# Expert rows of a mixture-of-experts stage added to their tokens by TensorE in PSUM, nine expert buffers in place of seven

## The chip, the core and the metric

The kernel runs on one NeuronCore of a Trainium2 chip. The metric is the device time of one execution in microseconds (us), here the median of three runs of the same program. The profile is of a fourth execution, taken by the hardware profiler; its clock starts at the first instruction.

## What is computed

One decoder layer for T = 320 tokens (256 of a prompt, 64 = 8 sequences of 8 new tokens), width 1024, all in fp32. First a mixer (a convolution group and a state-space group side by side, then one output projection), then a mixture of experts, then a last RMSNorm. The change touches the mixture of experts and the end:

```
t   = rmsnorm(x)                                   # 320 rows of 1024
grp = argmax(t @ rg_w + rg_b)                      # one of 4 groups
top 2 of the group's 8 experts, weights g1 * softmax(top 2)
for e in range(32):
    hid = silu(t @ w_gate[e]) * (t @ w_up[e])      # w_gate, w_up: 1024 x 512
    acc = acc + combine[:, e:e+1] * (hid @ w_down[e])   # w_down: 512 x 1024
y   = rmsnorm(x + acc)
```

Each token goes to 2 of 32 experts, so an expert has 20 tokens on average (640 pairs of token and expert over 32). A weight matrix of an expert holds 2 MiB, an expert three of them, all 32 experts 96.

## The kernel before

Everything is written by hand with semaphores, engine by engine; no scheduler reorders it. `S("name")` is a semaphore, `wait_ge` a wait, `then_inc` the count that an instruction adds when it is done. SP (SyncE) issues all weight loads from one queue, in order. `ring` holds six 2 MiB buffers through which first the mixer's weights and then the experts' weights go.

**The experts' weights.** `expert_units` (line 61) lists the 96 matrices in the order gate 0, up 0, gate 1, up 1, down 0, gate 2, up 2, down 1, and so on to gate 31, up 31, down 30, down 31. They are called units here, numbered 0 to 95; up 31 is unit 93. `e_slot` (line 362) has seven buffers: the six of the ring and `last_gate`, a piece of region_b. Unit j goes to buffer j mod 7 and is issued (line 440) when the unit seven before it has been used: after `gu_done` (gate and up product of an expert finished) or `dn_done` (down product finished).

**Routing.** After the output projection, VectorE (DVE) ranks the experts, gives each pair of token and expert a slot (at most CAP = 64 slots per expert), and TensorE turns that into lists by slot with a small product of 0/1 matrices (`slot_values`, line 1054): `gidx` (which row to gather), `sidx` (where to scatter), `wsl` (the weight of the slot).

**The expert loop.** GpSimd gathers the rows of expert e from `hn_dram` (line 677) into `gat`, an indirect DMA. TensorE (PE) then does for each expert, in this order: `gate_up(e)`, 16 products of 128x64 by 128x512 in pairs (lines 1079 and 1080, gate to partitions 0 to 63 of a PSUM bank and up to 64 to 127); `tokens_T(e+1)`, 8 transposes of the next expert's rows (line 1069); `down(e-1)`, 8 products (line 1091); `hidden_T(e)`, 4 transposes (line 1085). ScalarE (ACT) takes silu (line 1350), DVE multiplies and copies (helper line 1386). Each of these four products has two PSUM banks of its own, by even and odd expert, so all eight banks are used. `weigh(e)` (DVE, line 1717) multiplies the 64 rows of an expert by their weights into `yo`; one 128x512 tile, rows 0 to 63 with columns 0 to 511 of the result and rows 64 to 127 with columns 512 to 1023.

**Back to the tokens.** GpSimd scatters `yo` to `ye_dram` (line 682), where each token has two places, one for its first and one for its second expert. When all scatters have landed, GpSimd counts `ye_all` (line 721), SP reloads the 320 tokens' rows of both experts into the ring (line 510), and DVE adds both to `xt` (`add_experts`, line 1386 by the helper). Then the last RMSNorm: square on ACT (line 1367), square root on ACT (line 1370), reciprocal on DVE (line 1765), scaling on DVE (line 1387 by the helper), output by SP (line 514).

A branch for more than 64 tokens in one expert exists on every engine; each engine reads `mcount` into a register (`value_load`) behind the loop and jumps over it.

## Time and profile before

| | us |
|---|---|
| median of 3 runs | 903.55 |
| the runs | 900.63, 903.55, 903.62 |
| the profiled execution | 905.3 |
| its span, first to last instruction | 903.5 |
| PE busy | 768.4 (85%) |
| DVE, ACT, POOL busy | 300.5, 116.8, 191.2 |
| DMA, all queues | 254.54 MB, 282 GB/s over the span |

### The profile page before, as it was taken

The page shows a single profiled execution, that of the slowest core. Times are in us where ns is not written, and L with a number is a line of the kernel's source. Part 1 is how long each engine was busy: PE and PEld are TensorE (multiplying, and loading weights), DVE is VectorE, ACT ScalarE, POOL GpSimd, SP SyncE. Part 2 cuts the span into 40 slices and gives each one's busy share as a digit, 9 for nine tenths or more (in the row PEclk, how much of TensorE's full clock was granted, in tenths as well). Part 3 has the DMA queues.
Part 4 walks back from the last instruction along what each step waited for, and adds up shares of the span by engine and source line. Part 5 has one row for each costly group of instructions (what it writes and reads, how often), then busy time and mean ns, then how long its engine had stood idle before and what let it go on. Part 6 is the DMA issues. An engine that isn't in the chain of part 4 may idle for free.

```text
span 903.5 us, 8844 instructions
## 1 busy us (share of the span) xinstructions
PE 768.4 (85%) x3474; PEld 388.6 (43%) x3474; DVE 300.5 (33%) x662; ACT 116.8 (13%) x247; POOL 191.2 (21%) x219
## 2 busy tenths in 40 slices
PE   4999999989999996599987988798797797977970
PEld 3777677777533335343333332333242332333320
DVE  2079999952666114411111110101111011110105
ACT  3200211245410011000000000000000000000002
POOL 2088997310020002011111110101110111111010
PEclk9999999999999996589999988998898999989995
DMA  9882300216072994059999999999999999999915
GB/s 276 323 297 95 110 1 1 67 34 187 24 240 62 296 398 175 3 207 403 420 422 407 419 414 418 401 426 416 397 415 407 408 417 425 407 420 411 399 47 174
DMA packets 53544, 254.54 MB, mean 282 GB/s; under 512 B 8993, under 2 KB 26433, under 8 KB 40879
## 3 DMA queue, kind: packets, MB, share of 16 engines
q1 hardware_dynamic: 44948, 245.37, 68.9%
q0 software_dynamic: 5264, 5.40, 2.0%
q10 hardware_dynamic: 3291, 3.20, 1.2%
q8 instruction: 28, 0.46, 0.2%
q14 instruction: 13, 0.11, 0.0%
HBM read 248.96 MB, written 17.00 MB: 294 GB/s over the span
## 4 chain that ended last, share of the span: by engine, by line
PE 83%; issue 9%; DVE 5%; ACT 2%; DMA 1%; POOLq 0%; ACTq 0%; SPq 0%; DVEq 0%
PE bank L1079 27%; PE bank L744 18%; PE bank L1091 13%; PE bank L996 8%; PE bank L1069 4%; PE bank L1085 2%; PE bank L1080 1%; DVE region_a L1386 1%; PE bank L1041 1%; PE bank L826 1%; PE bank L969 1%; DMA ring<-ye_scratch 1%; PE bank L985 1%; PE bank L960 1%; DVE xt L1386 1%
## 5 line engine op out<-in xcount | busy, mean ns | idle before, releaser
L1079 PE MATMUL bank<-ring,region_a 128*64 128x512 f32 x432 | 216.9, 661 | 53.5 <-issue 52.6
L1080 PE MATMUL bank<-ring,region_a 128*64 128x512 f32 x432 | 217.5, 662 | 0.0
L744 PE MATMUL bank<-region_a,ring 128*128 128x320 f32 x576 | 158.9, 437 | 0.5 <-DVE region_a L1386 0.5
L1079 PEld LDWEIGHTS bank<-ring,region_a 128*64 128x64 f32 x432 | 63.1, 152 | 176.8 <-issue 176.3
L1386 DVE TENSOR_TENSOR zz<-zz,bank 64x512 f32<-64x512 f32 x32 | 22.1, 690 | 341.1 <-ACT zz L1350 341.1
L744 PEld LDWEIGHTS bank<-region_a,ring 128*128 128x128 f32 x576 | 109.9, 192 | 46.6 <-issue 2.1
L1091 PE MATMUL bank<-ring,region_a 128*64 128x512 f32 x448 | 102.3, 598 | 0.5 <-issue 0.5
L1387 DVE SCALAR_TENSOR_TENSOR bank<-region_a,par,bank 128x256 f32<-128x256 f32 x232 | 91.2, 481 | 0.0
L1080 PEld LDWEIGHTS bank<-ring,region_a 128*64 128x64 f32 x432 | 63.2, 152 | 0.0
L682 POOL DMA_INDIRECT ye_scratch<-yt,region_a x32 | 32.4, 1014 | 145.1 <-DVE yt L1717 141.3
L1350 ACT ACTIVATE zz<-bank 64x512 f32<-64x512 f32 x32 | 18.9, 592 | 335.5 <-PE bank L1080 335.5
L677 POOL DMA_INDIRECT vv<-hn_scratch,region_a x16 | 15.4, 963 | 194.4 <-PE bank L1069 168.6
L1079 PE MATMUL bank<-region_b,region_a 128*64 128x512 f32 x80 | 40.0, 657 | 15.4 <-issue 15.3
L1091 PEld LDWEIGHTS bank<-ring,region_a 128*64 128x64 f32 x448 | 30.2, 136 | 50.5 <-issue 48.8
L1717 DVE TENSOR_SCALAR yt<-bank,region_a 128x512 f32<-128x512 f32 x32 | 24.0, 750 | 83.6 <-PE bank L1091 83.6
L677 POOL DMA_INDIRECT yt<-hn_scratch,region_a x15 | 14.3, 956 | 126.0 <-PE bank L1069 126.0
L1080 PE MATMUL bank<-region_b,region_a 128*64 128x512 f32 x80 | 39.8, 656 | 0.0
L996 PE MATMUL bank<-ring,yt 128*128 128x512 f32 (+1 forms) x96 | 37.9, 603 | 0.0
L996 PE MATMUL bank<-ring,vv 128*128 128x512 f32 (+1 forms) x96 | 37.6, 608 | 0.0
L578 POOL TENSOR_TENSOR xt<-xt 128x512 f32<-128x512 f32 x29 | 36.8, 1269 | 2.3
L576 POOL TENSOR_TENSOR xt<-region_a,par 128x512 f32<-128x512 f32 x30 | 32.3, 1077 | 1.9
L1353 ACT ACTIVATE region_a<-bank 128x256 f32<-128x256 f32 x32 | 12.3, 384 | 144.0 <-PE bank L1085 144.0
(302 smaller groups left out, 699.0 us busy)
## 6 DMA issues: line engine op xcount, KB each, us to landing
ring<-in_expert_w_down SPq DMA_DIRECT2D x28, 2048.0 KB, 27.8
ring<-in_expert_w_gate SPq DMA_DIRECT2D x27, 2048.0 KB, 28.4
ring<-in_expert_w_up SPq DMA_DIRECT2D x27, 2048.0 KB, 23.1
ring<-in_w_in SPq DMA_DIRECT2D x9, 2048.0 KB, 20.2
region_b<-in_expert_w_gate SPq DMA_DIRECT2D x5, 2048.0 KB, 29.7
region_b<-in_expert_w_up SPq DMA_DIRECT2D x5, 2048.0 KB, 22.8
ring<-in_w_out SPq DMA_DIRECT2D x4, 2048.0 KB, 9.1
region_b<-in_expert_w_down SPq DMA_DIRECT2D x4, 2048.0 KB, 28.4
```

The source lines that it names most:

```text
L576: link(pool.tensor_tensor(tmp4, u_seq[:, :, :, k:k + TB], w4(par, k, NC), ALU.mult))
L578: return link(pool.tensor_tensor(acc, acc, tmp4, ALU.add))
L677: pool.indirect_dma_start(gat[e % 2], None, hn_dram[:, :], bass.IndirectOffsetOnAxis(ap=gidx[0:CAP, e:e + 1], axis=0), bounds_check=T - 1, ...
L682: pool.indirect_dma_start(ye_dram[:, :], bass.IndirectOffsetOnAxis(ap=sidx[:, e:e + 1], axis=0), yo[e % 2], None, bounds_check=4 * T - 1, ...
L744: ins = pe.matmul(pt[0:m, 0:T], w[:, k, :], ht[:, k, :], start=k == 0, stop=k == KD - 1)
L996: return pe.matmul(dst, mix, w, start=c == 0, stop=c == 2 * NC - 1)
L1069: ins = pe.transpose(bank[2 + b][:, CAP * k:CAP * k + CAP], gat[b][:, k:D:KD], ident[0:CAP, 0:CAP])
L1079: pe.matmul(bank[b][0:CAP, :], xgt[b][:, k, :], wg[:, FE * k:FE * k + FE], **st)
L1080: ins = pe.matmul(bank[b][CAP:P, :], xgt[b][:, k, :], wu[:, FE * k:FE * k + FE], **st)
L1091: ins = pe.matmul(bank[6 + b][CAP * q:CAP * q + CAP, :], hidt[b][:, k, :], wd[:, D * k + 512 * q:D * k + 512 * q + 512], start=k == 0, sto ...
L1386: tt_ = lambda out, a, b, op: dve.tensor_tensor(out, a, b, op)
L1387: stt = lambda out, a, s_, b, op0, op1: dve.scalar_tensor_tensor(out=out, in0=a, scalar=s_, in1=b, op0=op0, op1=op1)
```

## The change

1. **Adding by TensorE.** The scatter, `ye_dram` and the reload are gone. DVE makes for each expert a 0/1 matrix `back` (`places`): row s has a one in the column of the token that slot s holds. TensorE multiplies `yo` by it and adds up over all 32 experts in five PSUM banks, `acc` (`to_tokens`, `combine`): three tiles of tokens (128, 128, 64) times two column halves, six products per expert. The q = 0 product takes rows 0 to 63 of `back` and `yo`, the q = 1 product rows 64 to 127. For the two tiles of 128 tokens they write two different banks, for the tile of 64 tokens partitions 0 to 63 and 64 to 127 of one bank. `add_experts` reads `acc`.
2. **PSUM.** The four products of the loop have three banks for all experts in place of eight: `b_gu`, `b_t` (both transposes), `b_dn`.
3. **Nine expert buffers.** region_a and a piece of `xcx` are added; `hn`, `gat`, `hidt` and `yo` lie elsewhere (`vy`).
4. **Slots spread.** The number of a slot is no longer its partition: slots 0 to 15 of an expert are on the even partitions 0 to 30, slots 16 to 31 on the odd ones between them, 32 to 63 likewise above.
5. **Smaller.** One of the three value lists of the slots is gone (no `sidx`); the load of `gfin` is issued at expert 2.

```diff
-        gat = [t[0:CAP, D:2 * D] for t in (yf, vf)]
-        last_gate = rb[:, 0:UNIT]
+        gat = [vy[0:CAP, 3 * D + D * b:4 * D + D * b] for b in range(2)]
...
+        b_gu, b_t, b_dn = bank[0], bank[1], bank[2]
+        acc = bank[3:8]
...
-        e_slot = [ring[:, (N_MIX + m) % R, :] for m in range(2)] + [last_gate]
-        e_slot += [ring[:, (N_MIX + m) % R, :] for m in range(2, R)]
+        mix_slot = [ring[:, (N_MIX + m) % R, :] for m in range(R)]
+        e_slot = [xcx[:, 0:UNIT], mix_slot[0], rb[:, 0:UNIT]] + mix_slot[1:] + [ra[:, 0:UNIT]]
...
+                if c == 4:
+
+                    sp_.wait_ge(S("y_done"), 1)
+                    load_expert(0)
                 if c == 5:
 
                     sp_.wait_ge(S("h0_out0"), 64)
-                    load_expert(0)
+                    load_expert(1)
...
+            load_expert(2)
             sp_.wait_ge(S("h0_out1"), 64)
-            load_expert(1)
-            sp_.wait_ge(S("y_done"), 1)
-            load_expert(2)
+            load_expert(3)
             for m in range(2, R):
                 slot_free(N_MIX + m)
-                load_expert(m + 1)
+                load_expert(m + 2)
+            sp_.wait_ge(filled, J[("lg",)] + 1)
+            load_expert(n_slot - 1)
...
-            sp_.wait_ge(S("ye_all"), 1)
-            sp_.wait_ge(S("dn_done"), NE)
-            ye_tok = ye_dram.rearrange("(t c) n -> t (c n)", c=4)
-            for r, (t0, n) in enumerate(TILES):
-                sp_.dma_start(ring[0:n, r, 0:2 * D], ye_tok[t0:t0 + n, :]).then_inc(S(f"ye_in{r}"), 16)
...
-            pool.iota(slotno[:, :].rearrange("p (a s) -> p a s", a=2), [[0, 2], [1, CAP]], base=0,
-                      channel_multiplier=0, allow_small_or_imprecise_dtypes=True)
+            for a in range(2):
+                pool.iota(slotno[:, CAP * a:CAP * a + CAP].rearrange("p (h j i) -> p h j i", h=2, i=2),
+                          [[CAP // 2, 2], [1, CAP // 4], [CAP // 4, 2]], base=0,
+                          channel_multiplier=0, allow_small_or_imprecise_dtypes=True)
...
-            for e in range(NE + 2):
-                if e + 2 < NE:
-                    pool.wait_ge(S("xg_T"), e + 1)
-                    gather(e + 2)
-                if e >= 2:
-                    pool.wait_ge(S("yo"), e - 1)
-                    scatter(e - 2)
+            for e in range(NE - 2):
+                pool.wait_ge(S("xg_T"), e + 1)
+                gather(e + 2)
...
+            def to_tokens(b, r, first=False, end=False):
+                t0, n = TILES[r]
+                for q in range(2):
+                    dst = acc[2 * r + q][:, :] if r < 2 else acc[4][TS * q:TS * q + TS, :]
+                    ins = pe.matmul(dst, back[b][CAP * q:CAP * q + CAP, t0:t0 + n], yo[b][CAP * q:CAP * q + CAP, :],
+                                    start=first, stop=end)
+                return ins
+
+            def combine(e):
+                pe.wait_ge(S("yo"), e + 1)
+                for r in range(3):
+                    ins = to_tokens(e % 2, r, first=e == 0)
+                ins.then_inc(S("added"), 1)
...
-                wait(pe, S("hid"), e - 1)
+                wait(pe, S("hid"), e)
                 gate_up(b, gate, up).then_inc(S("gu_done"), 1)
...
                 if e + 1 < NE:
                     pe.wait_ge(S(f"gath{1 - b}"), 16 * ((e + 2) // 2))
-                    wait(pe, S("xgt"), e)
+                    wait(pe, S("hidt"), e)
                     tokens_T(1 - b).then_inc(S("xg_T"), 1)
+                if e >= 2:
+                    combine(e - 2)
                 if e:
                     w_down = expert_landed(pe, 2, e - 1)
                     pe.wait_ge(S("hidt"), e)
-                    wait(pe, S("yo"), e - 2)
+                    wait(pe, S("yo"), e - 1)
                     down(1 - b, w_down).then_inc(S("dn_done"), 1)
                 pe.wait_ge(S("hid"), e + 1)
-                wait(pe, S("hidt"), e - 1)
+                if e + 1 < NE:
+                    pe.wait_ge(S("xgt"), e + 2)
                 hidden_T(b).then_inc(S("hid_T"), 1)
+            combine(NE - 2)
+            over = pe.value_load(mcount[0:1, 0:1], min_val=0, max_val=T)
             w_down = expert_landed(pe, 2, NE - 1)
             pe.wait_ge(S("hidt"), NE)
-            pe.wait_ge(S("yo"), NE - 2)
             down(1, w_down).then_inc(S("dn_done"), 1)
-            over = pe.value_load(mcount[0:1, 0:1], min_val=0, max_val=T)
...
+            pe.wait_ge(S("yo"), NE)
+            for r in range(3):
+                to_tokens(1, r, end=True).then_inc(S("summed"), 1)
...
-                link(dve.tensor_scalar(col(M_E), tokid, 2.0, float(w) - BIG, ALU.mult, ALU.add))
-                tt_(val[w][:, :, 1, :], ee, wide(M_E, NE), ALU.mult)
-                link(tt_(val[w][:, :, 2, :], ee, wide(mw, NE), ALU.mult))
+                link(tt_(val[w][:, :, 1, :], ee, wide(mw, NE), ALU.mult))
...
+            def places(b, e):
+                return dve.tensor_scalar(back[b], tokno, gtok[:, e], None, ALU.is_equal)
+
             def weigh(e):
                 b = e % 2
+                wait(dve, S("added"), e - 1)
+                places(b, slice(e, e + 1)).then_inc(S("places"), 1)
                 dve.wait_ge(S("dn_done"), e + 1)
-                wait(dve, S(f"scat{b}"), 16 * (e // 2))
-                dve.tensor_scalar(yo[b], bank[6 + b][:, :], wsl[:, e:e + 1], None, ALU.mult).then_inc(S("yo"), 1)
+                dve.wait_ge(S("places"), e + 1)
+                dve.tensor_scalar(yo[b], b_dn[:, :], wsl[:, e:e + 1], None, ALU.mult).then_inc(S("yo"), 1)
...
             def add_experts(r):
                 n = TILES[r][1]
-                dve.wait_ge(S(f"ye_in{r}"), 16)
-                link(tt_(xt[0:n, r, :], xt[0:n, r, :], ring[0:n, r, 0:D], ALU.add))
-                tt_(xt[0:n, r, :], xt[0:n, r, :], ring[0:n, r, D:2 * D], ALU.add).then_inc(S("x3"), 1)
+                dve.wait_ge(S("summed"), r + 1)
+                for q in range(2):
+                    v = xt[0:n, r, 512 * q:512 * q + 512]
+                    ins = tt_(v, v, acc[2 * r + q][:, :] if r < 2 else acc[4][TS * q:TS * q + TS, :], ALU.add)
+                ins.then_inc(S("x3"), 1)
```

How the order on the engines changes. First PE in the expert loop, from the transposes of the next expert's rows to those of the hidden rows; before:

```order
L1069 MATMUL bank<-ident,yt 128x64 [waits s_xgt,s_gath0]
L1069 MATMUL bank<-ident,yt 128x64 x7
L1091 MATMUL bank<-ring,region_a 64x512 [waits s_yo,s_hidt,s_expert_in4]
L1091 MATMUL bank<-ring,region_a 64x512 x7
L1085 MATMUL bank<-ident,zz 128x64 [waits s_hidt,s_hid]
L1085 MATMUL bank<-ident,zz 128x64 x3
```

and now, at the same place (line 1050 is tokens_T, 1083 to_tokens, 1072 down, 1066 hidden_T):

```order
L1050 MATMUL bank<-ident,vy 128x64 [waits s_hidt,s_gath0]
L1050 MATMUL bank<-ident,vy 128x64 x7
L1083 MATMUL bank<-vy,zz 128x512 [waits s_yo]
L1083 MATMUL bank<-vy,zz 128x512 x3
L1083 MATMUL bank<-vy,zz 64x512 x2
L1072 MATMUL bank<-ring,vy 64x512 [waits s_yo,s_hidt,s_expert_in1]
L1072 MATMUL bank<-ring,vy 64x512 x7
L1066 MATMUL bank<-ident,zz 128x64 [waits s_xgt,s_hid]
L1066 MATMUL bank<-ident,zz 128x64 x3
```

Six products of the expert two before stand between the transposes and the down product.

Second, the end of the loop on PE now, from the last hidden transposes to the branch for full experts:

```order
L1066 MATMUL bank<-ident,zz 128x64 [waits s_hid]
L1066 MATMUL bank<-ident,zz 128x64 x3
L1083 MATMUL bank<-vy,region_a 128x512 [waits s_yo]
L1083 MATMUL bank<-vy,region_a 128x512 x3
L1083 MATMUL bank<-vy,region_a 64x512 x2
L1126 TENSOR_LOAD region_a
L1126 ISA x2
L1072 MATMUL bank<-ring,vy 64x512 [waits s_hidt,s_expert_in5]
L1072 MATMUL bank<-ring,vy 64x512 x7
L1130 COMPARE_AND_BRANCH
```

Before, the load of the register stood behind the last down product; now it and the six products of expert 30 stand ahead of it, and the six of expert 31 follow behind the branch.

Third, SP's queue where the loads that wait for the expert loop begin; before:

```order
L440 DMA ring<-in_expert_w_up 128x4096 [waits s_filled]
L440 DMA ring<-in_expert_w_down 128x4096 [waits s_gu_done]
L440 DMA ring<-in_expert_w_gate 128x4096 [waits s_gu_done]
L440 DMA region_b<-in_expert_w_up 128x4096 [waits s_gu_done]
L440 DMA ring<-in_expert_w_down 128x4096 [waits s_gu_done]
L440 DMA ring<-in_expert_w_gate 128x4096 [waits s_dn_done]
```

and now:

```order
L442 DMA ring<-in_expert_w_down 128x4096 [waits s_filled]
L442 DMA region_a<-in_expert_w_gate 128x4096 [waits s_filled]
L442 DMA xcx<-in_expert_w_up 128x4096 [waits s_gu_done]
L442 DMA ring<-in_expert_w_down 128x4096 [waits s_gu_done]
L442 DMA region_b<-in_expert_w_gate 128x4096 [waits s_gu_done]
L442 DMA ring<-in_expert_w_up 128x4096 [waits s_gu_done]
L442 DMA ring<-in_expert_w_down 128x4096 [waits s_dn_done]
```

The first load that waits for the loop is unit 9 (up 3) in place of unit 7 (down 1).

## Rows read from the trace of the kernel before

**Rows 1.** The page, part 2: DMA share and GB/s in 40 slices of 22.6 us.

```profile
DMA  9882300216072994059999999999999999999915
GB/s 276 323 297 95 110 1 1 67 34 187 24 240 62 296 398 175 3 207 403 420 422 407 419 414 418 401 426 416 397 415 407 408 417 425 407 420 411 399 47 174
```

**Rows 2.** Windows: length, busy time of PE to POOL, PEclk, DMA share, GB/s.

```profile
420.00:460.00 40.00, 37.34 (x184) 14.80 (x184) 7.15 (x10) 3.31 (x7) 6.95 (x7) 1.00 1.01 416
600.00:700.00 100.00, 82.25 (x372) 33.01 (x369) 13.54 (x19) 6.10 (x13) 11.84 (x12) 0.90 1.01 410
...
855.00:860.00 5.00, 2.33 (x14) 1.07 (x12) 0.75 (x1) 0.38 (x1) 0.99 (x1) 1.00 0.53 225
860.00:865.00 5.00, 5.00 (x19) 1.77 (x16) 0.00 (x0) 0.00 (x0) 0.00 (x0) 0.66 0.23 97
865.00:870.00 5.00, 5.00 (x26) 2.04 (x24) 0.69 (x1) 0.59 (x1) 0.00 (x0) 1.00 0.07 29
```

**Rows 3.** Timeline of PE, expert 1 and the start of expert 2.

```profile
396.04 0.61 PE L1079 MATMUL bank<-region_b,region_a 128*64 128x512 f32 x1
...
403.06 1.09 PE L1069 MATMUL bank<-ident,yt 64*128 64x64 f32 x8
404.08 3.65 PE L1091 MATMUL bank<-ring,region_a 128*64 128x512 f32 x16
407.66 0.69 PE L1085 MATMUL bank<-ident,zz 64*128 64x64 f32 x4
408.29 0.64 PE L1079 MATMUL bank<-ring,region_a 128*64 128x512 f32 x1
```

**Rows 4.** Timeline of PE, experts 29 and 31 and the last down product.

```profile
829.77 1.08 PE L1079 MATMUL bank<-region_b,region_a 128*64 128x512 f32 x1 [4.72 <-issue]
...
838.46 1.09 PE L1069 MATMUL bank<-ident,yt 64*128 64x64 f32 x8
...
859.39 0.61 PE L1079 MATMUL bank<-ring,region_a 128*64 128x512 f32 x1 [2.67 <-issue]
...
872.75 3.65 PE L1091 MATMUL bank<-ring,region_a 128*64 128x512 f32 x16 [0.52 <-issue]
```

**Rows 5.** Timeline of SP: the third load that waited for the loop.

```profile
403.16 0.33 SPq L440 DMA_DIRECT2D region_b<-in_expert_w_up  x1
```

**Rows 6.** The page, part 3: queue of the gathers and scatters.

```profile
q0 software_dynamic: 5264, 5.40, 2.0%
```

**Rows 7.** Timeline of PE: a pair of products on 32 rows each, and what follows.

```profile
296.12 1.13 PE L985 MATMUL bank<-region_b,xt 32*128 32x512 f32 x4
297.18 0.70 PE L996 MATMUL bank<-ring,vv 128*128 128x512 f32 x1
```

**Rows 8.** Groups of DVE from 365 to 880 us: busy us, mean ns of one.

```profile
L1717 DVE TENSOR_SCALAR yt<-bank,region_a 128x512 f32<-128x512 f32 x32 | 24.0, 750 | 83.6 <-PE bank L1091 83.6
L1386 DVE TENSOR_TENSOR region_a<-bank,lnffn 128x512 f32<-128x512 f32 x32 | 22.1, 692 | 2.2 <-PE bank L1069 1.2
...
L1386 DVE TENSOR_TENSOR region_a<-region_a 128x96 f32<-128x96 f32 x8 | 1.9, 256 | 0.2
...
L1673 DVE TENSOR_SCALAR region_a<-region_a 128x3 f32<-128x3 f32 x2 | 0.3, 160 | 0.0
```

**Rows 9.** The chain of waits, its last pieces: start, us, what.

```profile
877.97 2.32 DMA ye_scratch<-yt,region_a
881.73 0.97 POOLq L172
883.09 7.76 DMA ring<-ye_scratch
```

**Rows 10.** Timeline of DVE, the last norm.

```profile
893.28 0.15 DVE L1765 RECIPROCAL rst<-rst 128x1 f32<-128x1 f32 x1
...
894.67 2.46 DVE L1386 TENSOR_TENSOR xt<-xt,ring 64x1024 f32<-64x1024 f32 x2
```

**Rows 11.** Timeline of ACT, the last norm.

```profile
890.17 1.06 ACT L1367 ACTIVATE yt<-xt 128x1024 f32<-128x1024 f32 x1 [17.52 <-DVE xt L1386]
```

More of the change, by code:

```diff
@@ L304, in build @@
         gidx = moe(NE + 2).bitcast(I32)
[L305 removed]
+        gtok = moe(NE + 1)
         gcur = [moe(1).bitcast(I32) for _ in range(2)]
[L307 removed]
         mcount = moe(1).bitcast(I32)
@@ L1134, in _ @@
                     pe.wait_ge(S("sl_osel"), q + 1)
-                    slot_values(bank[0]).then_inc(S("sl_slots"), 1)
+                    slot_values(b_gu).then_inc(S("sl_slots"), 1)
                     wait_apart(pe, S("sl_idx"), q + 1)
@@ L1148, in _ @@
                         down(0, ring[:, 2, :]).then_inc(S("sl_dn"), 1)
+                        wait_apart(pe, S("sl_y"), n + 1)
+                        for r in range(3):
+                            ins = to_tokens(0, r)
+                        ins.then_inc(S("sl_back"), 1)
+            pe.wait_ge(S("yo"), NE)
+            for r in range(3):
+                to_tokens(1, r, end=True).then_inc(S("summed"), 1)
         @block.scalar
@@ L1722, in _ @@
                 wait(dve, S("hid_T"), e - 1)
-                tt_(hid[b], sil[b], bank[b][CAP:P, :], ALU.mult).then_inc(S("hid"), 1)
+                tt_(hid[b], sil[b], b_gu[CAP:P, :], ALU.mult).then_inc(S("hid"), 1)
                 if e + 1 < NE:
@@ L1742, in _ @@
                     dve.wait_ge(S("sl_slots"), q + 1)
-                    slot_indices(bank[0]).then_inc(S("sl_idx"), 1)
+                    slot_indices(b_gu).then_inc(S("sl_idx"), 1)
                     wait_apart(dve, S("sl_idx"), q + 1)
```

106 lines of the change are left out of this document (47 added, 59 removed).

## The prediction

> **What bounds the kernel now.** I read the slices of the page first. From slice 18 (407 us) to slice 37 (858 us) the DMA share is 9 and the rate near 415 GB/s [rows 1]: for half of the span the kernel does nothing but pour 96 weight matrices through the DMA engines. The windows say the same with PE beside it: from 420 to 460 us and from 600 to 700 us the share is 1.01, and PE is busy 82 of 100 us in the later window, at a granted clock of 0.90 [rows 2]. So PE has slack there, and the slack is what the change spends.
>
> How much slack: expert 1 starts at 396.04 and expert 2 at 408.29, with every weight there already; PE needs **12.25 us** for one expert [rows 3]. Expert 31 starts at 859.39 [rows 4], so 29 experts took (859.39 - 408.29) / 29 = 15.56 us each. The rest is waiting for weights: the idle 4.72 us ahead of expert 29 ended with no engine as releaser [rows 4]. On the DMA's side, unit 9 was issued at 403.16 [rows 5] and expert 31 could start, with unit 93, at 859.39: 85 units in 456.2 us, **5.37 us a unit**.
>
> Two things about the end. First, the DMA engines don't finish together: the share falls to 0.53 in 855 to 860, 0.23 in the next 5 us, and is still 0.07 (about one engine of 16) at 865 to 870 [rows 2]. A unit has landed only when the slowest engine has its part, so PE waits for that one. Second, the last down product starts at 872.75 and ends 3.65 us later, at 876.4 [rows 4], and the span ends at 903.5: a **tail of 27.1 us**, in which a scatter, a signal and a reload follow each other [rows 9] before the last norm can start.
>
> The sum is made against the profiled execution (span 903.5, its time 905.3); the median of the three runs is 903.55, and I take the same difference off it.
>
> **The change, part by part.**
>
> *Front.* Two 128x96 products (0.256) and two small scalings (0.160) leave DVE's serial list before the slots are chosen [rows 8]: 2 x 0.256 + 2 x 0.160 = 0.8 us earlier. The matrix of slot values has 64 columns in place of 96; I count nothing. Of the two loads more, one is issued at `y_done`, near 290 us (slices 12 and 13 at 62 and 296 GB/s), the other when the logits are there, near 355 us (slices 15 and 16 at 175 and 3 GB/s) [rows 1]: room for 5 us each. The more of iota and memset on GpSimd lies under the output projection. So expert 2 can start at 408.29 - 0.8 = 407.5.
>
> *PE per expert.* Six products more, that is 12 passes of 512 columns. Pairs of gate and up passes start about every 0.43 us (16 pairs in 403.06 - 396.04 = 7.02 us, the mode change at the end in it) [rows 3]. What decides is whether two products on *different rows* of the array run side by side as two on different columns do. The nearest row is the pair of line 985, on rows 0 to 31 and 32 to 63: its four passes take 297.18 - 296.12 = 1.06 us until the next product starts [rows 7]. One after the other they would need 4 x 0.43 = 1.72; side by side 2 x 0.43 = 0.86, and 0.2 is left for changing the array's division there and back. So I take six passes' time, 6 x 0.43 = 2.6, and 0.15 to 0.2 for the change between 128 and 64 columns: 2.75 us. Bounds: 2.57 (no drain) and 12 x 0.43 + 0.2 = 5.35 (no overlap on 64 rows). I stand near the lower end since that row has the same column count and type and differs in the rows alone. **PE's period becomes 12.25 + 2.75 = 15.0 us.**
>
> *DMA per unit.* Gathers and scatters took 2.0% of all engines' span [rows 6], 18 us; they move equal bytes, so the scatters are half, 9 us over 32 experts or 0.09 us a unit. 5.37 - 0.09 = 5.28 us. That the slowest engine gains more, since its share of slots is spread, I leave as a margin: bounds 5.08 (the lagging ends of rows 2 gone, and more) and 5.37 (nothing gained).
>
> *Nine buffers.* Nine units have landed before the loop in place of seven, in time that the DMA spent idle. The third load that waits for the loop is now unit 11, issued when expert 1's gate and up are done, at 403.16 - 0.8 = 402.4. Unit 93 is there after 83 units: 402.4 + 83 x 5.28 = **840.6**.
>
> *Which is last.* On PE expert 31 starts at 407.5 + 29 x 15.0 = **842.5**. PE is just later than the DMA, so the bound moves from the weights to PE, with the two only 2 us apart. The waits ahead of an expert, and with them the stretch at the lower clock after them, 1.2 in place of 2.4 GHz (granted 0.66 on average in 860 to 865 us [rows 2]; the gate and up of expert 29 took 838.46 - 829.77 = 8.7 us in place of 7.0 [rows 3, 4]), should nearly go.
>
> *Three PSUM banks for eight.* Every wait this adds has its work done long before: silu and the product on DVE read `b_gu` under the transposes and `down`; `yo` of the expert two before is ready some 7 us before `combine` asks. `places` is a 128x320 operation, between 0.26 (128x96) and 0.75 (128x512) [rows 8], in a DVE that waits 83.6 us in the loop for `down` alone; behind it in the queue stands `weigh`, which waits for `down` anyway. If PE's spare time were gone altogether these would still be 3 us or more from mattering.
>
> *From expert 31 to the last down product.* Gate and up 7.0, `combine` of 29 2.75, `down` 3.6, hidden transposes 0.65, `combine` of 30 2.75, the last `down` 3.65 [rows 3, 4]: 20.4 us. The register load between them has `combine` of 30 to hide under. 842.5 + 20.4 = 862.9.
>
> *Tail.* `weigh` 0.8 [rows 8]; products of tile 0: 0.86 and 0.25 to drain, 1.1; DVE's register load, once hidden under the reload, now ahead of the adds: below 1.44, the time from 880.29, when the scatter landed, to the signal at 881.73 on GpSimd, which holds the same load [rows 9], and I take 0.9 of it; two adds of 0.69 [rows 8], 1.4; from the square to the reciprocal 893.28 - 890.17 = 3.1 [rows 10, 11], then reciprocal and scaling 0.2 + 1.3; the adds of tile 2, 1.4; and from the end of those adds to the end of the span as before, 903.5 - 897.13 = 6.4 [rows 10]. Sum 16.6 in place of 27.1.
>
> **Sum:** 862.9 + 16.6 = 879.5 for the span, 24.0 less: 903.55 - 24.0 = **879.5 us** (881.3 for the profiled execution). Of the 24.0, 10.5 are the tail, and 13.5 that the last down product ends earlier.
>
> **Rivals.**
>
> *A. The DMA stays the bound.* If the slowest engine gains nothing from the scatters, unit 93 is there at 402.4 + 83 x 5.37 = 848.1; 5.6 us more, **885**. For: the two bounds are 2 us apart. Against: 9 us of work do leave the engines. 0.17.
>
> *B. Row pairs overlap, but each loses 0.1 us at its start* (line 985 has two such starts in 1.06 us), or gaps come between transposes and products: a period of 15.3 to 15.5, or 31 x 0.3 to 31 x 0.5 more, **889 to 895**. 0.08.
>
> *C. The pair for the last 64 tokens takes turns.* Its two products lie on different rows but write one bank; the pair of line 985 writes two banks, so no row shows this. Then two passes more, 0.86 us an expert: 842.5 + 29 x 0.86 = 867.4, then 22.1 and 17.1, **906.6**, a loss within what can be told. 0.03. The Trainium skill has a rule for it, in "TensorEngine Tiling (Array Packing)", gotcha on PSUM pressure: different row tiles cannot access one PSUM bank at the same time. By it this case would be certain if the hardware held one back.
>
> *D. Halves of 64 rows don't overlap at all* (slower than before). 12 passes in a row: period 17.6, expert 31 at 407.5 + 29 x 17.6 = 917.9, then 25.6 and 17.0, **960**. It decides from a `combine` of about 3.7 us on: there 407.5 + 29 x 15.95 + 22.3 + 16.6 reaches 909, over 0.5% above before. Against it speaks the pair of line 985 [rows 7]. 0.05.
>
> A rule that would make the DMA the bound: the Trainium skill, "DMA: Bandwidth & Descriptors", specifications, gives some 358 GB/s from HBM for one core. By that figure 83 units of 2.1 MB would take an estimated 486 us, unit 93 would come at 888 and the change gain little beyond the tail. The trace moves 410 to 416 GB/s over whole windows [rows 2], so the measurement decides against it.
>
> **How the numbers follow.** The forecast has 0.67: it is good from 873 (a `combine` of 2.57, no register load in the tail) to 886. The range takes in A and B and ends at B's upper end: **872 to 896**; C, D and what I haven't thought of are left out. Some 0.5%, 4.5 us, is what a measurement of this kernel can tell from no change. Faster by more than that: the forecast, A and B, 0.91 with the rest of 1 shared out; within it 0.03 (C); slower 0.06 (D and some unnamed wait).
>
> **What would show it.** In the profile after: experts start every 15.0 us from expert 2 to 31, with hardly a wait and a granted clock of 1.00; `to_tokens` (line 1083) takes 2.6 to 2.8 us from its first start to that of `down`; DMA share a little below 1.0 in the late windows; the first load that waits for the loop is one of up 3; tail of 16 to 17 us. Waits of microseconds ahead of an expert would speak for A; a `combine` of 3.1 to 3.3 for B, 3.6 for C, 5.3 for D. The forecast is wrong if the period isn't between 14.8 and 15.3 or the tail is above 19.

## The result, and the profile after

| | before | after |
|---|---|---|
| median of 4 runs, us | 902.09 | 879.4 |
| the runs | 897.69 to 903.62 | 878.73 to 880.73 |
| the profiled execution: time, span | 905.3, 903.5 | 880.73, 879.0 |
| expert 2 starts | 408.29 | 406.96 |
| expert 31 starts | 859.39 | 842.64 |
| last down product ends | 876.4 | 863.66 |
| tail from there | 27.1 | 15.3 |

The ratio is 0.9749, 95% interval 0.972 to 0.9778: 22.7 us faster by the medians. Forecast were 879.5 us and a range of 872 to 896, from a sum that takes 24.0 us off 903.55. Between the two profiled executions it is 24.5 us: 12.7 by which the last down product ends earlier, 11.8 of the tail.

The page of the changed kernel, parts 2 and 3, beside [rows 1] and [rows 6]:

```profile
PE   4999999989999999389999999999999999999994
...
PEclk9999999999999999579999999999999999999998
DMA  9892200036063798329999999999999999999921
...
q0 software_dynamic: 2704, 2.77, 1.2%
```

Windows of the changed kernel (columns as in [rows 2]):

```profile
420.00:460.00 40.00, 40.00 (x198) 15.78 (x195) 5.81 (x10) 2.93 (x6) 1.86 (x2) 1.00 1.01 420
600.00:700.00 100.00, 100.00 (x482) 39.02 (x478) 15.30 (x25) 6.70 (x14) 5.57 (x6) 1.00 1.01 410
835.00:840.00 5.00, 5.00 (x27) 2.34 (x28) 1.67 (x3) 0.34 (x1) 0.00 (x0) 1.00 0.91 387
840.00:845.00 5.00, 5.00 (x26) 1.90 (x24) 0.75 (x1) 0.38 (x1) 0.00 (x0) 1.00 0.15 62
845.00:850.00 5.00, 5.00 (x25) 1.59 (x22) 0.00 (x0) 0.23 (x1) 0.00 (x0) 1.00 0.00 0
```

From 600 to 700 us PE is busy 100 of 100 us, where it was busy 82, and its granted clock is 1.00, where it was 0.90. The DMA share is 1.01 as before, so a share near one doesn't say which of the two bounds. The waits do: of PE's waits before, 23 ahead of a gate and up product, ended by no engine, made 67.9 us, and now the list has none of this kind (one of 0.9 us ahead of expert 0 ends with DVE). The line is from the list before:

```profile
PE bank L1079 <- issue: 67.9, 23, 5.7
```

The loop is now one period repeated. Timeline of PE in the changed kernel, experts 2 and 31, and the end:

```profile
406.96 0.64 PE L1060 MATMUL bank<-ring,xcx 128*64 128x512 f32 x1
...
842.64 0.64 PE L1060 MATMUL bank<-region_b,vy 128*64 128x512 f32 x1
...
849.66 2.99 PE L1083 MATMUL bank<-vy,zz 64*128 64x512 f32 x12
852.58 3.65 PE L1072 MATMUL bank<-ring,vy 128*64 128x512 f32 x16
856.17 0.69 PE L1066 MATMUL bank<-ident,zz 64*128 64x64 f32 x4
857.09 2.99 PE L1083 MATMUL bank<-vy,region_a 64*128 64x512 f32 x12 [0.23 <-DVE vy L1728]
860.01 3.65 PE L1072 MATMUL bank<-ring,vy 128*64 128x512 f32 x16
864.52 2.99 PE L1083 MATMUL bank<-vy,zz 64*128 64x512 f32 x12 [0.86 <-DVE vy L1728]
```

(842.64 - 406.96) / 29 = 15.02 us an expert, and every one of the 29 periods is 15.02 or 15.03. The added products take 852.58 - 849.66 = 2.92 us from start to start, 12 passes. In the steady loop the first of them starts among the transposes ahead of it:

```profile
444.03 0.98 PE L1050 MATMUL bank<-ident,vy 64*128 64x64 f32 x7
444.75 0.69 PE L1083 MATMUL bank<-vy,region_a 64*128 64x512 f32 x1
444.85 0.27 PE L1050 MATMUL bank<-ident,vy 64*128 64x64 f32 x1
444.96 2.94 PE L1083 MATMUL bank<-vy,region_a 64*128 64x512 f32 x11
447.83 3.65 PE L1072 MATMUL bank<-ring,vy 128*64 128x512 f32 x16
```

The tail on DVE and ACT, where [rows 9 to 11] had a scatter, a signal and a reload:

```profile
863.71 0.75 DVE L1728 TENSOR_SCALAR vy<-bank,region_a 128x512 f32<-128x512 f32 x1 [6.39 <-PE bank L1072]
865.77 2.48 DVE L1394 TENSOR_TENSOR xt<-xt,bank 128x512 f32<-128x512 f32 x4 [1.30 <-PE bank L1083]
869.87 0.16 DVE L1780 RECIPROCAL rst<-rst 128x1 f32<-128x1 f32 x1 [1.63 <-ACT rst L1378]
...
871.27 1.38 DVE L1394 TENSOR_TENSOR xt<-xt,bank 64x512 f32<-64x512 f32 x2
872.57 0.15 DVE L1780 RECIPROCAL rst<-rst 128x1 f32<-128x1 f32 x1
```

```profile
867.08 1.06 ACT L1375 ACTIVATE vy<-xt 128x1024 f32<-128x1024 f32 x1 [9.81 <-DVE xt L1394]
...
868.25 1.28 ACT L1378 ACT_TABLE_LOAD   x1
```

Two things to take from these lines. DVE's first add waits for PE's product (1.30 us, released by L1083), not for the register load. And the loading of a function table for the square root (1.28 us) stands in the chain, as it did before the change (1.28 us at 891.33).

### The profile page after: what moved, and what is told of

It is laid out like the page before. It is cut to its first block, busy times and chain, and to the rows that moved or that the text cites. A ratio compares the mean times of both kernels' runs of the same rounds, so it can differ in the third digit from the quotient of the medians.

```text
span 879.0 us, 9574 instructions
## 1 busy us (share of the span) xinstructions
PE 826.7 (94%) x3858; PEld 405.1 (46%) x3858; DVE 305.8 (35%) x690; ACT 116.7 (13%) x247; POOL 157.9 (18%) x186
## 3 DMA queue, kind: packets, MB, share of 16 engines
q0 software_dynamic: 2704, 2.77, 1.2%
## 4 chain that ended last, share of the span: by engine, by line
PE 91%; DVE 5%; ACT 2%; issue 1%; DMA 0%; ACTq 0%; DVEq 0%
PE bank L1060 26%; PE bank L725 18%; PE bank L1072 13%; PE bank L1083 10%; PE bank L977 8%; PE bank L1050 3%; PE bank L1066 2%; PE bank L807 1%; DVE region_a L1394 1%; PE bank L950 1%; PE bank L966 1%; PE bank L1022 1%; PE bank L941 1%; PE bank L914 1%; PE bank L1097 0%
## 5 line engine op out<-in xcount | busy, mean ns | idle before, releaser
L1072 PE MATMUL bank<-ring,vy 128*64 128x512 f32 x512 | 116.9, 598 | 0.0
L1061 PE MATMUL bank<-ring,xcx 128*64 128x512 f32 x176 | 80.5, 611 | 0.0
L1061 PE MATMUL bank<-ring,vy 128*64 128x512 f32 x176 | 79.3, 604 | 0.0
L977 PE MATMUL bank<-ring,vy 128*128 128x512 f32 (+1 forms) x192 | 75.5, 606 | 0.0
L1072 PEld LDWEIGHTS bank<-ring,vy 128*64 128x64 f32 x512 | 33.9, 136 | 80.0 <-issue 80.0
L1083 PE MATMUL bank<-vy,zz 64*128 64x512 f32 (+1 forms) x192 | 50.1, 611 | 0.9 <-DVE vy L1728 0.9
L1083 PE MATMUL bank<-vy,region_a 64*128 64x512 f32 (+1 forms) x192 | 50.3, 611 | 0.2 <-DVE vy L1728 0.2
L1060 PE MATMUL bank<-region_b,vy 128*64 128x512 f32 x96 | 43.9, 612 | 0.0
L1050 PEld LDWEIGHTS bank<-ident,vy 64*128 64x128 f32 x256 | 30.6, 200 | 27.5 <-issue 25.2
L1050 PE MATMUL bank<-ident,vy 64*128 64x64 f32 x256 | 35.0, 277 | 1.5 <-DVE vy L1714 1.5
L1060 PE MATMUL bank<-ring,vy 128*64 128x512 f32 x80 | 35.4, 595 | 0.0
L1060 PE MATMUL bank<-region_a,xcx 128*64 128x512 f32 x80 | 35.4, 595 | 0.0
```

The costliest lines, as they stand in the source:

```text
L977: return pe.matmul(dst, mix, w, start=c == 0, stop=c == 2 * NC - 1)
L1050: ins = pe.transpose(b_t[:, CAP * k:CAP * k + CAP], gat[b][:, k:D:KD], ident[0:CAP, 0:CAP])
L1060: pe.matmul(b_gu[0:CAP, :], xgt[b][:, k, :], wg[:, FE * k:FE * k + FE], **st)
L1061: ins = pe.matmul(b_gu[CAP:P, :], xgt[b][:, k, :], wu[:, FE * k:FE * k + FE], **st)
L1072: ins = pe.matmul(b_dn[CAP * q:CAP * q + CAP, :], hidt[b][:, k, :], wd[:, D * k + 512 * q:D * k + 512 * q + 512], start=k == 0, stop=k == 3)
L1083: ins = pe.matmul(dst, back[b][CAP * q:CAP * q + CAP, t0:t0 + n], yo[b][CAP * q:CAP * q + CAP, :], start=first, stop=end)
```

## The experiments

The prediction had come out, so the question was which of its reasons hold. Four were open: that PE now bounds and by how much, that the row halves overlap, what each side change is worth, and why the DMA's bound lies where it does. Twelve runs followed, two of them repeats. One number is used throughout, the **unit time**: from the issue of the third load that waits for the loop to the start of expert 31, over the units between (85 with seven buffers, 83 with nine). It is the DMA's pace only where PE waits for the weights.

### no_combine

```diff
             def combine(e):
+                if e:
+                    return
...
-                wait(dve, S("added"), e - 1)
+                wait(dve, S("added"), 1 if e >= 2 else 0)
```

> The changed kernel without the products that add an expert's rows to the tokens for experts 1 to 30 (they stay for expert 0 and 31, so y lacks the other experts); DVE no longer waits for them. Theory (PE's bound and the weights' are only some 2 us apart): PE's period falls back to 12.25 us while landed weights last, then PE waits for weights again; expert 31 starts near 838 to 842 us as with the products, and only the two sets of products behind it (2 x 2.9 us) and the tail stay saved: 871 to 874. Rival 1 (the DMA has much slack beside a PE bound): a unit at 5.1 us or less, expert 31 before 830, 860 or less. Rival 2 (the products cost nothing since the DMA was the bound all along): 879.

Measured: 866.37 us, ratio 0.9603 (0.9571 to 0.9635). The loop is bound by the weights again. (Besides the lines shown, the wait for `added` in the branch for full experts is left out.) Neither expectation came: expert 31 starts at 832.98, between the theory's 838 to 842 and rival 1's 830. SP's queue, PE's timeline and PE's waits in this kernel:

```profile
399.93 0.33 SPq L442 DMA_DIRECT2D region_b<-in_expert_w_gate  x1
```

```profile
803.61 0.81 PE L1060 MATMUL bank<-ring,vy 128*64 128x512 f32 x1 [4.15 <-issue]
...
804.21 1.06 PE L1060 MATMUL bank<-ring,vy 128*64 128x512 f32 x1
...
805.06 1.06 PE L1060 MATMUL bank<-ring,vy 128*64 128x512 f32 x1
...
832.98 0.61 PE L1060 MATMUL bank<-region_b,vy 128*64 128x512 f32 x1 [2.37 <-issue]
```

```profile
PE bank L1060 <- issue: 49.9, 21, 4.9
```

The unit time is (832.98 - 399.93) / 83 = **5.22 us**. In the changed kernel unit 11 is issued at 401.85, so unit 93 could be used at 401.85 + 83 x 5.22 = 835.1: the DMA is 7.5 us ahead of PE's 842.64, where I forecast 2. The middle lines show what a wait costs beside itself: after 4.15 us of idle the pairs start 0.85 us apart, twice the 0.43 of the full clock. The changed kernel never pays that.

The slack can be checked at the end of the stream of weights. Windows of 1 us, first of the changed kernel, then of no_combine:

```profile
840.00:841.00 1.00, 1.00 (x6) 0.29 (x4) 0.00 (x0) 0.00 (x0) 0.00 (x0) 1.00 0.50 213
```

```profile
839.00:840.00 1.00, 1.00 (x8) 0.48 (x6) 0.00 (x0) 0.00 (x0) 0.00 (x0) 1.00 0.50 213
```

The share is down to a half 1 us later in the changed kernel. If unit 93 lies as far ahead of that point in both, it had landed by 832.98 + 1 = 834, and the slack is 8.7 us. The two ways agree to about 1 us; 7.5 is used below.

PE is the later one only as long as the lead of landed weights lasts. Three units take 3 x 5.22 = 15.66 us, more than PE's 15.02 for an expert, which is why the DMA share stays at 1.01. The lead shrinks by 0.64 us an expert: at expert 4, which starts at 437.01 and needs unit 12, it is 437.01 - (401.85 + 2 x 5.22) = 24.7 us, at expert 31 7.5. An estimate from these figures: after some 12 more experts the weights would bound again.

### same_rows

Both products of a pair take rows 0 to 63, so nothing but the rows differs.

```diff
-                    ins = pe.matmul(dst, back[b][CAP * q:CAP * q + CAP, t0:t0 + n], yo[b][CAP * q:CAP * q + CAP, :],
+                    ins = pe.matmul(dst, back[b][0:CAP, t0:t0 + n], yo[b][0:CAP, :],
```

> The changed kernel with both products of a pair on rows 0 to 63 of the matrix and of the weighted rows, so that they can't lie on different rows of the array (the sums are then of wrong halves). Theory (the change pays because 64-row halves run side by side): for the four products of 128 columns the passes take turns, 8 x 0.43 in place of 4 x 0.43; the last two (64 columns each, different column halves, same rows) may still overlap. 1.7 us an expert more if they do, 2.6 if not: period 16.7 to 17.6, 931 to 960 us. Rival (the row halves never ran side by side, or PE isn't the bound): 879.

Measured: 933.02 us, ratio 1.0344 (1.0302 to 1.0385). PE's timeline:

```profile
430.75 4.66 PE L1083 MATMUL bank<-vy,zz 64*128 64x512 f32 x12
435.34 3.65 PE L1072 MATMUL bank<-ring,vy 128*64 128x512 f32 x16
```

The 12 passes take 435.34 - 430.75 = 4.59 us in place of 2.92, and the period is (891.52 - 406.06) / 29 = 16.74 in place of 15.02; 29 x 1.72 = 50, with 3.4 more from expert 31 to the last down product and 0.9 in the tail, and the medians differ by 53.6. Four passes more would be 4 x 0.43 = 1.72: the two pairs with 128 columns take turns, and the pair for the last 64 tokens, which still uses different columns, does not. That is the theory's lower case. So the rows alone let the pairs overlap, and the change lives on it: without it, it loses 3.4%.

### slots_in_order and seven_buffers

Two side changes are undone, each alone in the changed kernel: first the spread of the slots.

```diff
-            for a in range(2):
-                pool.iota(slotno[:, CAP * a:CAP * a + CAP].rearrange("p (h j i) -> p h j i", h=2, i=2),
-                          [[CAP // 2, 2], [1, CAP // 4], [CAP // 4, 2]], base=0,
+            pool.iota(slotno[:, :].rearrange("p (a s) -> p a s", a=2), [[0, 2], [1, CAP]], base=0,
```

> The changed kernel with slot s on partition s again (slots not spread). Theory A (PE is the bound, the DMA 2 us ahead): a lag of the slowest engine of some us comes back, as the gathers' rows lie on few engines; 2 us of it are hidden: 879 to 883. Theory B (the spread is what took the lag of about 10 us away): 885 to 889, with DMA shares falling step by step over 10 us at the end of the weights. Theory C (it does nothing, the scatters made the lag): 879, and the weights end as sharply as in the changed kernel (0.91, then 0.15 in 5 us windows).

Then the two more buffers, with the order of the first loads that goes with seven.

```diff
-        e_slot = [xcx[:, 0:UNIT], mix_slot[0], rb[:, 0:UNIT]] + mix_slot[1:] + [ra[:, 0:UNIT]]
+        e_slot = mix_slot[0:2] + [rb[:, 0:UNIT]] + mix_slot[2:]
```

> The changed kernel with the seven buffers and the order of loads of the kernel before. Theory (the two bounds meet only because nine units are there at the start): the DMA becomes the bound, unit 93 lands two units later, 10.5 us less 2 us of slack: 886 to 889. Rival (the scatters' absence alone speeds the DMA enough): 879 to 881.

Measured: slots_in_order 879.81 us, ratio 0.9754 (0.9714 to 0.9794), no difference from the changed kernel that can be told; its period is (841.95 - 406.27) / 29 = 15.02. Its DMA windows at the end:

```profile
840.00:845.00 5.00, 5.00 (x26) 1.84 (x24) 0.75 (x1) 0.38 (x1) 0.00 (x0) 1.00 0.37 157
845.00:850.00 5.00, 5.00 (x26) 1.72 (x24) 0.30 (x1) 0.59 (x1) 0.00 (x0) 1.00 0.04 16
```

Where the changed kernel has 0.15 and 0.00, the shares are 0.37 and 0.04: some of the lag between the engines is back, as theory A says and theory C denies, and the slack covers it. By the 5.26 us a unit of before_no_scatter below, an estimate, 83 units from about 401 us on end near 838, still 4 us ahead of PE.

seven_buffers 884.01 us, 0.9808 (0.9767 to 0.9848), between what theory (886 to 889, with 2 us of slack) and rival (879 to 881) gave. Its experts start every 15.0 us until about expert 20 and then up to 16.3 apart, on average (844.79 - 406.18) / 29 = 15.12. The last wait for weights is ahead of expert 29, which needs unit 87, and there the unit time is (814.75 - 401.06) / 79 = 5.24, the DMA's own (no_combine has (803.61 - 399.93) / 77 = 5.24 ahead of the same expert): two buffers fewer are two units of lead, 10.4 us, more than the 7.5 us of slack. Waits for weights are back, small ones:

```profile
PE bank L1055 <- issue: 2.5, 4, 1.2
```

29 x 0.10 = 2.9 us of the 4.6 between the medians are this, and 10.4 - 7.5 = 2.9 is what the slack leaves; the rest lies within what runs and the front differ by.

### before_spread, before_no_scatter and spread_no_scatter

The same question on the side where the weights bound: each in the kernel before, then both. The spread is the edit above turned round. The scatters are left out with

```diff
-                if e >= 2:
+                if e >= NE:
                     pool.wait_ge(S("yo"), e - 1)
                     scatter(e - 2)
```

> The kernel before with only the slots spread over the partitions as in the change (slot s on even, then odd partitions). The DMA is the bound there, so whatever the spread gives the slowest engine shows. Theory S (the lag of about 10 us between the engines comes from slots 0 to 20 lying on few engines, in gathers and scatters alike): expert 31 starts some 6 to 9 us earlier, 893 to 897. Theory N (the spread gives next to nothing, as with the changed kernel, where slots in order cost nothing): 900 to 903.

> The kernel before without the scatters of experts 0 to 29 (those of 30 and 31 and the tail's chain stay; the rows added at the end are read from weights of the same size, so y is wrong). Theory 1 (with the scatters gone a unit takes 5.2 us as in the changed kernel, mean load and the slowest engine's together): expert 31 starts near 403 + 85 x 5.2 = 845, 14 us earlier, 887 to 890. Theory 2 (only their mean load goes, 0.09 us a unit): 8 us earlier, 893 to 895. Theory 3 (the gain in the DMA came from the memory layout or the buffers): 901.

> The kernel before with the slots spread and without the scatters of experts 0 to 29 (y wrong, as in before_no_scatter). Each alone gave 7 to 9 us. Theory O (both take work off the same slowest engines, so together they give little more than one: the unit reaches 5.2 us as in the changed kernel): 888 to 891. Theory P (they act apart and add): 885 or less.

Measured:

| | median, us | ratio (95%) | unit time | DMA share falls below 0.5 in |
|---|---|---|---|---|
| before | 902.09 | 1 | (859.39 - 403.16) / 85 = 5.37 | 860 to 865 |
| spread alone | 893.9 | 0.992 (0.9889 to 0.9952) | (847.12 - 398.78) / 85 = 5.27 | 855 to 860 |
| no scatters alone | 892.59 | 0.9906 (0.9874 to 0.9937) | (848.10 - 401.07) / 85 = 5.26 | 850 to 855 |
| both | 888.23 | 0.9853 (0.9827 to 0.988) | (844.59 - 401.33) / 85 = 5.21 | 850 to 855 |

How the engines end, by windows: first the spread alone, then no scatters alone, then both.

```profile
850.00:855.00 5.00, 5.00 (x26) 1.68 (x24) 0.12 (x1) 0.59 (x1) 0.00 (x0) 1.00 0.62 256
855.00:860.00 5.00, 4.48 (x24) 1.74 (x22) 1.32 (x2) 0.38 (x1) 0.78 (x1) 1.00 0.01 3
```

```profile
845.00:850.00 5.00, 4.27 (x24) 1.75 (x21) 0.75 (x1) 0.38 (x1) 0.00 (x0) 1.00 0.73 308
850.00:855.00 5.00, 5.00 (x26) 1.92 (x24) 0.00 (x0) 0.00 (x0) 0.00 (x0) 1.00 0.34 144
```

```profile
845.00:850.00 5.00, 5.00 (x18) 1.91 (x16) 0.00 (x0) 0.00 (x0) 0.00 (x0) 0.66 0.94 397
850.00:855.00 5.00, 5.00 (x26) 2.01 (x24) 0.69 (x1) 0.59 (x1) 0.00 (x0) 1.00 0.21 88
```

The spread alone gave theory S (893 to 897), both together theory O (888 to 891); the scatters alone, at 892.59, lie just under theory 2's 893 to 895 and far from theory 1. Read ahead of experts 29, 30 and 31 of one kernel, the unit time differs by 0.02 to 0.03.

Spreading the slots takes nothing off the DMA: queue 0 moves 5264 packets and 5.40 MB as in [rows 6]. Yet it takes 0.10 us off a unit, and where the share faded over three windows (0.53, 0.23, 0.07 in [rows 2]) it now drops from 0.62 to 0.01. So where the small rows lie is worth as much as all the scatters. The two overlap: against the kernel before on the same chip (901.2, 901.2 and 900.47 us) they gain 7.3, 8.6 and 12.2 us, and both together less than the sum of 15.9. That fits scatters which load the slowest engine most, so that each edit takes part of what the other would. Which of the 16 engines is the slowest, and how a slot's partition leads to it, no view shows; that link stays argued. There is a rival for part of it: with the spread the packets under 512 bytes are 8681 in place of 8993, so the scatters' bytes are cut into packets otherwise, and no run separates that from the placing. For the gathers it is separated: without scatters the two counts are 7179 and 7195, and the spread still takes the unit time from 5.26 to 5.21.

The figures fit together: 5.21 with neither scatters nor lag in the memory layout and seven buffers of before, and 5.22 and 5.24 in no_combine and seven_buffers, which have neither. **The DMA's bound in the changed kernel is 5.22 us a unit.**

### tail_order, tail_again and changed_again

A root of a spare number loads ACT's function table ahead of the end, and the adds of the last 64 tokens go ahead of the first scaling.

```diff
+            act.activation(rst[:, 6:7], rst[:, 7:8], ACT.Sqrt)
...
-            final_norm(0)
             add_experts(2)
+            final_norm(0)
```

> The changed kernel with two edits behind the experts: DVE adds all three tiles before it scales the first, and ScalarE takes a square root of a constant first, so that its table is there before the norm. Theory (the tail is a chain of DVE and ACT work in which the table load of 1.28 us and the scaling ahead of the last adds both lie): the last square starts at some 869.5 in place of 872.7; 1.5 to 2.5 us faster than the changed kernel, 877 to 878. Rival (the output of the first tile, later by a microsecond or so, or DVE's order makes up for it): 879.

> The kernel of tail_order once more. Its profile had a tail of 13.4 us in place of 15.3, and expert 2 1.5 us later than in the changed kernel's profile. Theory (the tail's 1.9 us are real and a late start hid them): 1 to 3 us below changed_again. Rival (something in the kernel makes the start later): the same time as changed_again, expert 2 again later by 1.5 us.

> The changed kernel once more, to compare the next two with it on one chip: 878 to 881. The start of expert 2 differs from profile to profile (403.9 to 410.9 us so far), so this run also shows how much of a difference of a microsecond or two the front makes by itself.

tail_again is tail_order once more, and changed_again the changed kernel, on one chip. Measured: tail_order 879.86 us (ratio 0.9756, 0.9731 to 0.9782), tail_again 878.25 (0.9762, 0.9734 to 0.979), changed_again 881.3 (0.9779, 0.9753 to 0.9805). The tail is 878.6 - 865.2 = 13.4 and 874.2 - 860.8 = 13.4 us in place of 15.3; ACT in tail_again goes from the square to the root with no load between:

```profile
864.20 1.06 ACT L1376 ACTIVATE vy<-xt 128x1024 f32<-128x1024 f32 x1 [7.72 <-DVE xt L1395]
865.16 0.19 ACT L1376 ACTIVATION_READ_ACCUMULATOR vy<-xt 128x1 f32 x1
865.38 0.29 ACT L1379 ACTIVATE rst<-ssq 128x1 f32<-128x1 f32 x1
```

1.9 us in both profiles; the two edits weren't tried apart. The medians are 0.5 us above the changed kernel's (theory 1.5 to 2.5 below) and 3.1 us below changed_again's (theory 1 to 3 below), and the intervals overlap, so by the whole time it stays unclear. Why: the front alone differs by more. Expert 2 starts at 408.48 in tail_order and 404.06 in tail_again, the same kernel. Windows of tail_order:

```profile
380.00:390.00 10.00, 9.12 (x34) 3.58 (x35) 0.69 (x1) 0.00 (x0) 0.94 (x1) 0.66 0.02 5
390.00:400.00 10.00, 8.80 (x40) 3.56 (x38) 1.38 (x2) 0.97 (x2) 0.93 (x1) 0.83 0.73 272
```

and of tail_again:

```profile
380.00:390.00 10.00, 9.63 (x40) 3.77 (x40) 0.55 (x2) 0.59 (x1) 0.94 (x1) 0.82 0.03 6
390.00:400.00 10.00, 8.80 (x47) 3.86 (x48) 1.47 (x3) 0.97 (x2) 0.93 (x1) 1.00 1.01 395
```

The clock comes back from 1.2 to 2.4 GHz after the thin stretch of the routing (granted 0.50 from 355 to 375 us in both) earlier in one execution than in the other: expert 0 takes 12.8 or 11.5 us and expert 1 13.9 or 12.2, together 3.0 of the 4.4 us. The other 1.4 stand already at the start of expert 0 (381.77 and 380.37), and no run tells why.

### halves_bf16 and halves_and_tail

If PE is later by 7.5 us, cheaper products should give just that. DVE splits the weighted row into two bf16 parts (the rounded value and the rest), and both go through the same 0/1 matrix, in bf16 too: 12 products of one pass in place of six of two, at the price of a second operation on DVE and of precision: the two parts keep some 16 bits of a weighted row.

```diff
-        yo = [vy[:, 512 * b:512 * b + 512] for b in range(2)]
+        yo = [[vy[:, 512 * b + 256 * i:512 * b + 256 * i + 256].bitcast(BF16) for i in range(2)] for b in range(2)]
...
-                for q in range(2):
...
+                for i in range(2):
+                    for q in range(2):
...
-                dve.tensor_scalar(yo[b], b_dn[:, :], wsl[:, e:e + 1], None, ALU.mult).then_inc(S("yo"), 1)
+                link(dve.tensor_scalar(yo[b][0], b_dn[:, :], wsl[:, e:e + 1], None, ALU.mult))
+                stt(yo[b][1], b_dn[:, :], wsl[:, e:e + 1], yo[b][0], ALU.mult, ALU.subtract).then_inc(S("yo"), 1)
```

> The changed kernel with the weighted rows split by DVE into a bf16 part and a bf16 remainder, and the 0/1 matrix in bf16, so that each fp32 product is two bf16 products (their sum keeps some 16 bits). Theory (PE is the bound, the DMA has 9 to 10 us of slack as the run without the products showed, and a bf16 pass of 512 columns takes about half of an fp32 pass): the products take 1.5 to 1.7 us in place of 2.9, PE's period 13.7 to 13.9; the weights become the bound again, expert 31 starts near 833 to 835; two sets of products behind it are shorter by 2.6 together and a DVE operation of 0.75 is added on the path twice: 868 to 872. Rival 1 (a bf16 pass is no faster than an fp32 pass here): 879 to 882. Rival 2 (DVE's second operation delays the products): 873 to 880.

> halves_bf16 and tail_order together. Theory (one edit acts in the expert loop, where the weights are the bound then, the other behind it, so they add): tail 13.4 us less 0.6, 868 to 871, 9 to 11 us below changed_again. Rival (they don't add): 872.

Measured: halves_bf16 872.3 us, ratio 0.9669 (0.9634 to 0.9704); with the edit of the tail, halves_and_tail, **868.42 us, 0.9639 (0.9616 to 0.9662)**, the fastest of the kernels that leave nothing out, 11.0 us under the changed kernel and 12.9 under changed_again on the same chip, where 9 to 11 were expected. halves_bf16 alone is 7.1 us under the changed kernel, 0.3 above the end of its theory's range. PE's timeline of halves_bf16:

```profile
845.88 1.59 PE L1085 MATMUL bank<-vy,zz 64*128 64x512 bf16 x12
847.39 3.65 PE L1073 MATMUL bank<-ring,vy 128*64 128x512 f32 x16
```

and of halves_and_tail:

```profile
837.29 0.61 PE L1061 MATMUL bank<-region_b,vy 128*64 128x512 f32 x1 [0.81 <-issue]
...
851.13 1.59 PE L1085 MATMUL bank<-vy,region_a 64*128 64x512 bf16 x12 [1.02 <-DVE vy L1398]
```

The products take 847.39 - 845.88 = 1.51 us in place of 2.92. The period is 13.7 for the first 14 experts, and then the weights bound; on average (837.29 - 408.61) / 29 = 14.78, and the unit time, from SP's issue at 403.50, is (837.29 - 403.50) / 83 = 5.23. That is the bound that no_combine showed, reached with all the adding done; halves_bf16 has (838.86 - 405.78) / 83 = 5.22. What DVE's second operation costs shows at the end, where PE waits 1.02 us in the line above (0.23 in the changed kernel) and 1.65 ahead of the last products (0.86). So the tail of halves_and_tail is 869.9 - 856.3 = 13.6 us and not the expected 12.8: there DVE's operation takes back all that the cheaper products give.

## Why the prediction was right, step by step

- **Front.** Forecast 0.8 us earlier, measured 1.3 (408.29 to 406.96). The 1.3 are two things: expert 0 starts 3.4 us earlier (384.09 to 380.72), and experts 0 and 1 take 26.2 us in place of 24.2, with a granted clock of 0.83 from 390 to 400 us where it was 1.00. Between profiles of one kernel the start of expert 2 moves by 4.4, so the step is neither confirmed nor refuted.
- **PE's period.** Forecast 12.25 + 2.75 = 15.0, measured 15.02. Expert 31 was forecast at 842.5 and starts at 842.64, by luck that close: the front is 0.5 us earlier and 29 periods 0.7 us longer than forecast. The pair of line 985 [rows 7] was the right row; same_rows shows that the overlap is by rows.
- **Nine buffers.** The third load was forecast at 402.4, issued at 401.85. It was right to count the lead of two units: with seven buffers the weights bound again.
- **DMA per unit: mis-sized.** "5.37 - 0.09 = 5.28 us" with the slowest engine's gain left "as a margin". Measured 5.22. I took the scatters at their mean load, 0.09, and they are worth 0.11 (before_no_scatter); for the spread I took nothing, and it is worth 0.10 alone and 0.05 on top. Over 83 units this made "the two only 2 us apart" where they are 7.5 apart; 0.5 of the difference is the earlier issue of unit 11. The bounds, 5.08 and 5.37, held it. It did not move the forecast, since PE was later either way, but rival A got 0.17 on the strength of those 2 us.
- **Waits and the clock.** Forecast that they nearly go; 67.9 us of waits went, and the granted clock is 1.00 from 420 us on.
- **Three banks, `places`.** Forecast at nothing, and that is shown: no_combine keeps both, and its experts 4 to 9 start 12.25 us apart (432.32, 493.55), as in the kernel before.
- **From expert 31 to the last down product.** Forecast 20.4, measured 863.66 - 842.64 = 21.0: 0.23 us of waiting for `weigh` of expert 30, which I had not listed, and 2 x 0.17 since `combine` from start to start is 2.92 here and not 2.75. In the steady loop, where it overlaps the transposes, it adds 15.02 - 12.25 = 2.77.
- **Tail: mis-sized.** Forecast 16.6, measured 15.3. The 0.9 us for DVE's register load was wrong: from the end of `down` to the first add are 865.77 - 863.66 = 2.1 us, all of it `weigh` and the products, where I had 0.8 + 1.1 + 0.9 = 2.8. From there to the first reciprocal are 4.1 us (forecast 1.4 + 3.1), then 1.4 to the adds of tile 2 (1.5), 1.3 for them (1.4), and 879.0 - 872.57 = 6.4 to the end (6.4).
- **Signs.** The period, the granted clock, the missing waits and the first load that waits, one of up 3, are as I said. Three signs are not. From the first `to_tokens` product to `down` are 447.83 - 444.75 = 3.1 us in the loop and 2.92 at expert 31, where I gave 2.6 to 2.8, and 3.1 to 3.3 for B; the first product starts ahead of the last transpose, so the distance misleads, and the period decides against B. The tail is 15.3, not 16 to 17. And the DMA share is 1.01, not a little below 1.0: by my own figures three units need 3 x 5.28 = 15.8 us, more than PE's 15.0, so the DMA had no reason to rest.
- **Rivals.** A, B and D did not come, D being what same_rows comes near to by force. C did not come either: the pair for the last 64 tokens writes one bank from different row tiles, and 12 passes in 2.92 us are 6 x 0.43 + 0.34. Had it taken turns, 0.86 us more would show. So the rule of the Trainium skill, "TensorEngine Tiling (Array Packing)", gotcha on PSUM pressure, is not borne out in time here, where the two write partitions 0 to 63 and 64 to 127 of the bank.
- **The rate of the DMA.** 410 and 420 GB/s over whole windows also after the change. The Trainium skill's 358 GB/s ("DMA: Bandwidth & Descriptors", specifications) does not fit that. The same page of the Trainium skill, in its section on bandwidth, gives this figure for each core of a pair when both stream, and 425 GB/s as measured on one core alone; here one core ran.

The last down product ended 0.8 us later than forecast and the tail is 1.3 us shorter: 879.5 forecast and 879.0 measured for the span are closer than the terms are, by luck. So are 879.5 and 879.4 for the median: four runs of the kernel before have 902.09 and not 903.55, so 22.7 us stand against the 24.0 forecast, and changed_again had 881.3.

## What to carry to other kernels

When a kernel waits for a stream of weights, work can be moved onto the engine that waits, up to the slack; how much slack there is, is best read by leaving the added work out once, since the mean load of the DMA engines hides the one that is last. The slack can be a lead of landed buffers that is being used up, as here, and then it depends on how long the loop is. Two products on different row halves of the array run side by side, so moving rows by a 0/1 matrix of 64 rows costs 0.43 us for a pair of fp32 passes of 512 columns. When the bound has moved, side changes are worth less: the spread of the slots gave 7.3 us in the kernel before and nothing that can be told here, and of the 10.4 us of lead in two more buffers some 3 to 5 us show. The next gain lies in the new bound: here cheaper products, then the tail.

## What was not expected of the hardware

- The DMA engines' lag from a few rows on few partitions: 5.4 MB of 254.5, and laying them on other partitions shortens the whole by 7.3 us.
- The return of TensorE's clock varies from one execution of a kernel to the next and makes up 3.0 of the 4.4 us between starts of expert 2 at 404.06 and 408.48 us; a gain of 2 us can't be told in medians beside it, though each profile shows it.
- A pass of bf16 with 512 columns takes half the time of an fp32 pass: 12 passes in pairs in 1.51 us against 2.92, or 0.25 and 0.49 a pair, the change of the array's division in it.
